# Gate and up products of the FFN by seven block products in place of eight

## What is computed

```python
def block_output(x, h_m, h_a, w_out, ln1_g, ln1_b, w_gate, w_up, w_down, ln2_g, ln2_b):
    mix = jnp.concatenate([h_m, h_a], axis=-1).astype(x.dtype)
    x = layer_norm(ALPHA * x + mix @ w_out, ln1_g, ln1_b)
    ff = (jax.nn.silu(x @ w_gate) * (x @ w_up)) @ w_down
    return layer_norm(ALPHA * x + ff, ln2_g, ln2_b)
```

## Time and profile before

| | us |
|---|---|
| median of three runs (1586.88 to 1593.45) | 1587.2 |
| span of the profiled execution | 1586.6 |
| start of the FFN's matmuls (L1830) | 804.9 |
| start of the y stage (L1988) | 1521.9 |
| PE busy (share of the span) | 1546.0 (97%) |
| DVE, ACT, POOL busy | 772.3, 451.5, 412.3 |

### The profile page before, as it was taken

How to read it: one execution, slowest core, us unless ns; L and a number is a source line. 1 busy time by engine, 2 the same in 40 slices (tenths; PEclk the granted TensorE clock), 3 DMA queues, 4 the chain that set the end, 5 groups by cost and what they waited for, 6 DMA issues and landing times.

```text
span 1586.6 us, 26851 instructions
## 1 busy us (share of the span) xinstructions
PE 1546.0 (97%) x10593; PEld 1435.2 (90%) x10593; DVE 772.3 (49%) x1664; ACT 451.5 (28%) x929; POOL 412.3 (26%) x405
## 2 busy tenths in 40 slices
PE   7999999999999998899999999999999999999998
PEld 7986799999996666687899999999999999999986
DVE  2008599999965664563653323324132332313146
ACT  4336423222145564361352120221112012111100
POOL 3620256321110002453683221221122122112200
PEclk9999999999999999999999999999999999999999
DMA  5210231222317004543202101101111111111011
GB/s 187 72 44 19 65 101 41 71 83 85 104 46 258 28 27 130 161 128 123 67 27 80 53 27 54 54 30 51 54 54 27 54 54 36 45 54 54 1 61 76
DMA packets 117236, 110.52 MB, mean 70 GB/s; under 512 B 16218, under 2 KB 102366, under 8 KB 117122
## 3 DMA queue, kind: packets, MB, share of 16 engines
q1 hardware_dynamic: 116482, 106.80, 21.6%
q0 software_dynamic: 640, 2.10, 0.4%
HBM read 88.82 MB, written 19.95 MB: 69 GB/s over the span
## 4 chain that ended last, share of the span: by engine, by line
PE 58%; POOL 0%; DVE 0%; issue 0%; DVEq 0%
PE bank L1830 32%; PE bank L1808 13%; PE bank L1599 6%; PE bank L1993 3%; PE bank L1988 0%; PE bank L1748 0%; PE bank L1167 0%; PE bank L1595 0%; PE bank L1170 0%; POOL c_and_n_sample L1317 0%; PE bank L1133 0%; PE bank L1153 0%; PE bank L1182 0%; PE bank L1103 0%; POOL mv_by_sample L1313 0%
## 5 line engine op out<-in xcount | busy, mean ns | idle before, releaser
L1830 PE MATMUL bank<-x_split,gate_up_split 128*128 128x352 f32 x3168 | 509.9, 322 | 0.0
L1830 PEld LDWEIGHTS bank<-x_split,gate_up_split 128*128 128x128 f32 x3168 | 507.3, 188 | 0.1
L2284 PE MATMUL bank<-w_split,xT_split 128*128 128x256 f32 (+1 forms) x1950 | 247.7, 284 | 3.7 <-POOL w_split L2517 2.0
L2284 PEld LDWEIGHTS bank<-w_split,xT_split 128*128 128x128 f32 (+1 forms) x1950 | 234.3, 187 | 8.2 <-issue 3.7
L1911 DVE TENSOR_TENSOR hidden<-silu,bank 128x352 f32<-128x352 f32 x66 | 34.4, 521 | 408.5 <-ACT silu L1873 408.5
L1808 PE MATMUL bank<-hidden_split,weight_split 128*128 128x352 f32 x1296 | 209.2, 322 | 0.0
L1808 PEld LDWEIGHTS bank<-hidden_split,weight_split 128*128 128x128 f32 x1296 | 208.0, 188 | 0.0
L1947 POOL TENSOR_TENSOR gate_up_split<-gate_up,gate_up_split 128x2048 fp32r<-128x2048 f32 x22 | 104.1, 4734 | 370.7 <-ACT gate_up_split L1865 370.7
L2622 DVE TENSOR_SCALAR_CACHE_REDUCE chosen<-scores,level 128x384 uint8<-128x384 f32 (+2 forms) x198 | 174.3, 943 | 1.2
L1816 DVE TENSOR_TENSOR y_acc<-y_acc,bank 128x352 f32<-128x352 f32 x216 | 112.5, 521 | 84.6 <-PE bank L1808 83.4
L2341 PE MATMUL bank<-xT_split,w_split 128*128 128x352 f32 x864 | 138.4, 322 | 0.0
(11 more groups left out here) (310 smaller groups left out, 1703.3 us busy)
## 6 DMA issues: line engine op xcount, KB each, us to landing
w_unit<-in_w_in_dram SPq DMA_DIRECT2D x15, 1024.0 KB, 5.7
gate_up<-in_w_gate_dram SPq DMA_DIRECT2D x22, 512.0 KB, 4.0
gate_up<-in_w_up_dram SPq DMA_DIRECT2D x22, 512.0 KB, 5.2
down_weight<-in_w_down_dram SPq DMA_DIRECT2D x11, 1024.0 KB, 4.9
scratch_dram<-feature_stage SPq DMA_DIRECT2D x36, 176.0 KB, 1.8
scores<-in_x_prompt_dram SPq DMA_DIRECT2D x8, 512.0 KB, 3.9
out_dram<-stage SPq DMA_DIRECT2D x32, 128.0 KB, 1.7
out_weight<-in_w_out_dram SPq DMA_DIRECT2D x16, 256.0 KB, 6.2
```

Source lines behind the costliest of these rows:

```text
L1830: mm = pe.matmul(PS[2 * c + w][:, 0:CH], gs[u][:, a, w, k, :], xs[:, b, k, c * CH:(c + 1) * CH], start=(k == 0 and (a, b) == PARTS[0]), st ...
L2284: mm = pe.matmul(out, tokens, w[:, b, k, :], start=((k, a, b) == terms[0]), stop=((k, a, b) == terms[-1]))
```

## The change

Gate and up products are formed by a scheme of 2 x 2 blocks with seven block products (Winograd's form of Strassen's). The tokens are split in two halves of 528, K in two halves of four k blocks, a group's 256 weight columns in two blocks of 128. A matrix is now the gate or the up of one group (22 of them), and consists of seven products `j`, each with two pieces `c` of 272 and 256 token columns: 4 k x 3 parts = 12 matmuls a piece, 168 a matrix, in place of 144 of 352 columns. The stages on PE are gate g, down g - 1, up g.

- The sums of activations (`T1` to `T4`) are made once, for the second half of the tokens (tiles 4 to 7 and `LAST`): DVE forms them (`halves_of`), ACT copies highs (`sums_high`), POOL makes lows.
- The sums of weights are made for every matrix on DVE: `weight_sums` (three) and `last_weight_sum` (one). In a down they stand behind adds 15 and 18; in an up matrix, and in the gates 0 and 10, behind the third result piece and the last.
- The seven weight pieces of a matrix (128x512, four of them sums) go through a ring of four slots: ACT makes the high of a piece (`high_part`), three pieces ahead, POOL the low (`low_part`). The four pieces of a down use the same ring.
- Products 0 and 1 share a bank; ACT copies the first one out (`put_p1`) before the second is added to it. DVE combines the banks (`products_16`, `products_165`, `result`), ACT takes silu, DVE multiplies (`hide`) and splits (`split_hidden`).
- In the second out-projection sweep the tiles come in the order 0 to 3, LAST, 4 to 7, and a tile's transposes stand inside the next tile's product, behind 21 of its 24 matmuls. The last tile's transposes stand in the first matrix, whose pieces have an order of their own.
- The residual's scaling moves from POOL into the first down's adds. Machine loops are unrolled. The rows of the y stage come in another order, and the last down weights' lows are four operations of 128x1024.

```diff
+        HT = T // 2
+        CO, CW = (0, 272), (272, HT - 272)
...
+        RING_W = 4
...
+        for g in range(GROUPS):
+            stages += [("gate", g)] + ([("down", g - 1)] if 0 < g < GROUPS - 1 else []) + [("up", g)]
+        parts = [(kind, g, j) for kind, g in stages for j in range(4 if kind == "down" else 7)]
...
             for t in range(TILES):
                 add(1, t)
                 spread_of(t)
                 centre(t)
+                if t < LAST:
+                    if t:
+                        halves_of(t - 1)
+                    if t == LAST - 1:
+                        weight_sums(dve, 0)
...
+            for t in range(TILES - 3):
+                lows(t)
+            low_part(pool, 0)
+            low_part(pool, 1)
+            lows(TILES - 3)
+            low_part(pool, 2)
+            low_part(pool, 3)
+            low_part(pool, 4)
+            lows(TILES - 2)
+            low_part(pool, 5)
+            lows(TILES - 1)
...
+            for t in range(LAST):
+                if t:
+                    put_turned(2 * t - 2)
+                std(t)
+                if t:
+                    put_turned(2 * t - 1)
+                if t >= 2:
+                    sums_high(t - 2)
+            high_part(act, 0)
+            high_part(act, 1)
+            put_turned(2 * LAST - 2)
+            std(LAST)
+            put_p1(act, 0, 0)
+            put_turned(2 * LAST - 1)
+            put_p1(act, 0, 1)
+            sums_high(LAST - 2)
+            for e in (2, 3, 4):
+                high_part(act, e)
+            silu(act, 0, 0, 0)
+            silu(act, 0, 0, 1)
+            put_turned(2 * LAST)
+            put_turned(2 * LAST + 1)
+            high_part(act, 5)
+            sums_high(LAST - 1)
...
+            return (A11, A12, A11, A21, s1_sum, A12, A22)[j]
...
+                elif half == 0:
+                    before = part_no[("gate", "up")[(n - 1) % 2], (n - 1) // 2, 0]
+                    sp.wait_ge(summed, summed_no(n - 1, 5))
+                    sp.wait_ge(slot_lo, before + 4)
+                else:
+                    before = part_no[("gate", "up")[(n - 1) % 2], (n - 1) // 2, 0]
+                    sp.wait_ge(slot_lo, before + 7)
...
-                    for w in range(2):
-                        for k in range(KD):
-                            for a, b in PARTS:
-                                mm = pe.matmul(PS[2 * c + w][:, 0:CH], gs[u][:, a, w, k, :],
...
+        XPARTS = (B11, B21, T2, T3, T1, B22, T4)
+        BANK_OF = (0, 0, 2, 4, 2, 0, 4)
...
+                if j == 1:
+                    pe.wait_ge(p1_put, 2 * n + c + 1)
+                if j == 4:
+                    pe.wait_ge(combined, combined_no(n, "p16", c))
...
+                for k in range(4):
+                    for a, b in PARTS:
+                        mm = pe.matmul(PS[BANK_OF[j] + c][:, 0:CW[c]], slot(e, a)[:, k, :],
+                                       XPARTS[j][:, b, k, CO[c]:CO[c] + CW[c]],
...
+            def first_matrix():
+                for j in (0, 1):
+                    multiply(0, j, 0)
+                    multiply(0, j, 1)
+                pe_x1(pe, 2 * LAST)
+                pe_x1(pe, 2 * LAST + 1)
+                for c in range(2):
+                    for j in (2, 3, 4, 5):
+                        multiply(0, j, c)
+                multiply(0, 6, 0)
+                multiply(0, 6, 1)
...
+            def more(e):
+                if e + 3 < len(parts):
+                    high_part(act, e + 3)
...
+                n, e = stage_no_of(kind, g), part_no[kind, g, 0]
+                more(e)
+                put_p1(act, n, 0)
+                put_p1(act, n, 1)
+                for j in range(1, 7):
+                    more(e + j)
...
+            dve.tensor_tensor(s1, A21, A22, ALU.add).then_inc(summed, 1)
+            dve.tensor_tensor(A21, A11, A21, ALU.subtract).then_inc(summed, 1)
+            dve.wait_ge(slot_lo, e + 1)
+            dve.wait_ge(summed, summed_no(n, 3))
+            dve.tensor_tensor(A11, s1, A11, ALU.subtract).then_inc(summed, 1)
...
+                if sums_here:
+                    weight_sums(dve, n + 1)
+                result(dve, n, 3, 0)
+                result(dve, n, 3, 1)
+                if up:
+                    hide(g, 3, 0)
+                    hide(g, 3, 1)
+                    split_hidden(g, 3)
+                if sums_here:
+                    last_weight_sum(dve, n + 1)
...
+                    if m == 15:
+                        weight_sums(dve, 2 * g + 3)
+                    if m == 18:
+                        last_weight_sum(dve, 2 * g + 3)
```

More of the change, by code:

```diff
@@ L1499, in build @@
[L1499 to L1503 removed]
+        HT = T // 2
+        CO, CW = (0, 272), (272, HT - 272)
+        Q = 4 * HT
@@ L1504, in build @@
+        x_tm = [put(f"x_tm{i}", at, D) for i, at in enumerate(X_TM)]
+        y_tm = [put(f"y_tm{i}", TS0 + i * D if i < LAST else R0, D) for i in range(TILES)]
         wo = [put(f"out_weight_split{h}", at, 2 * KD * 512, F32R).rearrange("p (k s n) -> p k s n", k=KD, s=2)
@@ new lines, in dve_out @@
+            for t in range(TILES):
+                add(0, t)
+                if t < 2:
+                    mix_low(dve, LOW_BY_DVE[t + 2], mix_lo_dve)
+            for t in range(TILES):
+                add(1, t)
+                spread_of(t)
+                centre(t)
+                if t < LAST:
[3 more added lines that the diff above has]
+                        weight_sums(dve, 0)
+            dve.tensor_copy(s1_sum, s1_first).then_inc(summed, 1)
@@ new lines, in act_x1, with part_free @@
+            for c in range(2):
+                silu(act, 0, 1, c)
+                silu(act, 0, 2, c)
+            high_part(act, 6)
+            high_part(act, 7)
+            high_part(act, 8)
+            high_part(act, 9)
+            silu(act, 0, 3, 0)
+            silu(act, 0, 3, 1)
+        def part_free(eng, e):
+            if e >= RING_W:
+                kind, g, j = parts[e - RING_W]
+                if kind == "down":
+                    eng.wait_ge(d_ps, 3 * MD * g + 6 * (j + 1))
+                else:
+                    eng.wait_ge(product, product_no(stage_no_of(kind, g), j, 1))
+            else:
+                eng.wait_ge(norms["first"]["nT"], 2 * (6 + e))
@@ new lines, in act_ffn, with matrix, last_high @@
+        def act_ffn(act):
+            def more(e):
+                if e + 3 < len(parts):
+                    high_part(act, e + 3)
+            def matrix(kind, g):
+                n, e = stage_no_of(kind, g), part_no[kind, g, 0]
[4 more added lines that the diff above has]
+                    more(e + j)
+                    if kind == "gate" and j != 2 and j != 3:
+                        q = {1: 0, 4: 1, 5: 2, 6: 3}[j]
+                        silu(act, g, q, 0)
+                        silu(act, g, q, 1)
+                    if n == 2 * GROUPS - 1 and j in (4, 6):
+                        last_high((j - 4) // 2)
+            def last_high(u):
+                act.wait_ge(wd_in[u], 16 * (2 * (GROUPS - 2) + 1))
+                for k in range(2):
+                    act.activation(wl[u][:, 0, k, :], wl_raw[u][:, k, :], ACT.Copy).then_inc(slot_hi, 1)
+            for kind, g in stages[1:]:
+                if kind == "down":
+                    for j in range(4):
+                        more(part_no[kind, g, j])
+                else:
+                    matrix(kind, g)
@@ L2042, in sp_phase5 @@
                 dst = y_prompt[0, i * P:(i + 1) * P, :] if i < LAST else y_sample.rearrange("b t d -> (b t) d")
-                parts = 2 if t == LAST else 1
-                for half in range(parts):
-                    cols = slice(D // parts * half, D // parts * (half + 1))
-                    sp.wait_ge(nm["normed"], 2 * t + 2 // parts * (half + 1))
+                pieces = 2 if t == LAST else 1
+                for half in range(pieces):
+                    cols = slice(D // pieces * half, D // pieces * (half + 1))
+                    sp.wait_ge(nm["normed"], 2 * t + 2 // pieces * (half + 1))
                     sp.dma_start(dst[:, cols], y_tm[i][0:rows(i), cols]).then_inc(y_stored, 16)
@@ L2056, in act_phase5 @@
             act_out(act)
-            high(act, 0, 0)
             act_x1(act)
```

738 lines of the change are left out of this document (454 added, 284 removed).

## The result

| | before | after |
|---|---|---|
| median of twenty runs, us | 1589.5 | 1593.5 |
| ratio, with its 95% interval | | 1.0026 (1.0019 to 1.0034) |
| profiled span, us | 1586.6 | 1595.0 |
| PE busy | 1546.0 | 1507.1 |
| DVE, ACT, POOL busy | 772, 452, 412 | 977, 508, 509 |

The forecast was no difference, 1587; the runs show a small loss of 0.26%. Single runs of the two kernels overlap, but the interval of the ratio lies clear of 1. Of the 8.4 us between the two spans about five lie ahead of everything that was changed. So the runs' medians say how much slower the kernel is, and the profile is read from the out projection on.

The account below looks back on a forecast made before the run. PE, busy 97% of the span, was taken to bound the kernel. Terms: -56.9 + 10.3 + 12 + 32 + 2.9 = 0.3 us, so 1586.6 + 0.3 + 0.6 = 1587.5, given as 1587; 8-in-10 range 1566 to 1608.

Parts of the forecast that it names:

- The saving: Gate and up matrices on PE: 20.46 us in place of 23.05 each, 56.9 us saved over 22 matrices.
- The rival that the matmuls go at the slower pace: New gate and up matmuls run at the rate they have among transposes: 12.6 us less saved, 1600; chance 0.07.
- the one that width doesn't matter: Gate and up matmuls cost 160.07 ns whatever their width: +84.5 us, 1672; chance 0.01.
- The downs: Nine downs: three weight sums ahead of DVE's add 16 make PE wait 1.14 us each, 10.3 in all.
- the slack of 0.26: In a down, PE's slack at step 18, subtracted from add 16's lateness of 1.40 us to give 1.14.
- The turns: Ten turns from an up to the next gate: second product waits 1.2 us for ACT's copy, 12 us in all.
- The start: First matrix and beginning of the next: waits of 28.7 us plus 3.4 for lower clock, 32 us (26 to 39).
- Rival (5): In the start, no wait hides the lower clock: 6 x 1.7 us in place of 3.4, 1594; chance 0.07.
- The end: Last up matrix: POOL's lows of the last down weights delay DVE, the y stage waits 2.9 us (0 to 5).
- The likeliest case: Whole kernel: the forecast of 1587 us, no difference, own range 1579 to 1595; chance 0.30.
- Rival (1): POOL doesn't delay DVE's run in the up; turns and end lose nothing: 1572 us; chance 0.26.
- The Trainium skill's rule on the shared port: DVE and POOL operations on SBUF exclude each other for the whole instruction; third rival, 1596 us; chance 0.07.

Follow-up runs that it names:

- e2: Changed kernel with ACT's copies of a gate's first product ahead of the highs of weight pieces 2 and 3 at the ten turns: 1579.5 us, ratio 0.9934.
- e5: Changed kernel with POOL's low of piece 1 of each gate after the first cut to a quarter of its columns: 1585.3 us, ratio 0.9967.
- e6: Changed kernel with matmuls of unused result put into five long waits of the first matrix to keep PE busy: 1593.6 us, ratio 1.0030.

## Why the prediction failed by its sum, and held by its steps

No difference was forecast, and the runs show a loss of 4 us. The mechanisms told are in the traces at all four places; what failed are the sizes of terms: the slack in the downs, the restart behind a wait, and the way in which waits and half clock were added in the start.

**The saving** was right: -56.9 predicted, -57.9 measured. The line between two widths of another stage gave 125.3 and 118.3 ns; pieces of 272 and 256 in turn go at 121.5 on the mean (48 in 5.83, 867.96 to 873.79). The rival that the matmuls go at the slower pace, and the one that width doesn't matter, are out.

**The downs** are the first mis-sized term: 1.48 us each, 1.14 predicted. That add 16 comes late was right almost to the digit (1.48 for 1.40). The step that failed is the slack of 0.26 subtracted from it: it was worked out from the modelled end of a matmul and a guessed handing over. By starts, step 18 of the first down is due at 921.79 (18 steps of 0.962 from 904.48) and begins at 923.18, 1.39 late, so that the slack is 0.09; and the 36 matmuls behind it lose another 0.09. The wait of the record (1.21) is less than the loss; only the distance from start to start shows all of it.

**The turns** are the second: 1.43 each, 1.2 predicted. Their mechanism, with the POOL low in DVE's run and the sum at 23.0, stood as it was told, and e2 removes the loss, e5 a good half of it. From start to start the second product is 1.33 late (953.71, where 949.46 + 2.92 was due); the last 0.1 is lost behind it, as in the downs. Why a restart costs that 0.1 is open; the granted clock there is 1.00.

**The start** came out at 30.4 for 32, and that it came so near is in part luck. The prediction had eight waits of 28.7 us in all, at full clock, and added 3.4 for what no later wait hides of a lower clock. The record has six, 5.63, 5.92, 3.94, 2.43, 2.82 and 0.38, 21.1 in all, and 8.5 at half clock, in four stretches; behind the waits of 2.43 and 0.38 the clock is 1.00. The two waits at product 1 are not in it, since PE came there late, at half clock. The step that failed is the addition: half clock lengthens the stretches between waits and shortens the waits, and by e6 nearly all of it is hidden. The price of 1.7 us for one wait isn't shown by its rows either: in the trace of before the granted clock was down ahead of the wait of 2.25, too (PE busy, PEclk, DMA share, GB/s).

```profile
645.00:646.00 1.00, 1.00 (x4) 0.50 1.17 293
```

Rival (5), that nothing hides it, is out.

**The end** was 3.8 for 2.9, by the mechanism told.

The errors add up to 3.6 us (-1.0 + 3.0 + 2.3 - 1.6 + 0.9), on a forecast whose terms of 57 against 57 cancelled: the sign of such an answer depends on every small term. The likeliest case, no difference, is not what was measured, and none of the rivals is what happened. Most of the rest of the distance from 1587 to 1593.5 is the reference itself: three runs had a median of 1587.2, twenty have 1589.5. Rival (1), that POOL doesn't delay DVE, is out: cutting the one POOL low short (e5) gives 8.3 of the 14.3 us that the turns lose. The Trainium skill's rule on the shared port ("SBUF — State Buffer", "SBUF: two separate sides"), which would have made the sum higher, is borne out meeting by meeting: the multiplication at 944.69 ended at 946.14, 0.3 us behind POOL's low, the operation of 7.07 in e6 0.5 behind POOL's fifth low, and POOL's lows take 1.74 beside a dense DVE. But a term of the sum already held the meetings at the turns, and the sum didn't rise by the 9 us that I drew from it.

## What to carry to other kernels

A cheaper algorithm on the bound engine is worth what its new helpers' queues let through: price every instruction that an in-order queue puts ahead of the one the bound engine waits for, and look first at whether the order alone can be changed, since here the order (and, for 3 us, the engine of four operations) cost 43 of the 58 us that the new algorithm saves. Place one helper operation in each gap, not three in one, and not where the two engines that exclude each other meet. Measure losses from start to start of what repeats, not by the gaps that the record shows.

## What was not expected of the hardware

Stretches at half clock (8.5 us lost by the windows) cost little, about 1 us by the estimate at e6, since waits for other engines stood behind each. Two engines that meet on SBUF cost each other much at short notice: a multiplication of 0.42 takes 1.45, a low of 1.29 takes 1.74, and three groups of DVE's at the end lose 8 us to four POOL operations. The price was not the same each time: DVE's sums and POOL's lows for the last tile take turns in after, 1.5 to 1.8 each, and in e6 one DVE operation stands through five lows, 7.07.
